# The end of an fp32 encoder kernel: last weight tile in four blocks, last output half by fp32 products, final norm by halves of the columns

## The reference, cut to what matters

```python
def _rmsnorm(x, g):
    xf = x.astype(jnp.float32)
    y = xf * lax.rsqrt(jnp.mean(xf * xf, axis=-1, keepdims=True) + RMS_EPS)
    return (y * g.astype(jnp.float32)).astype(x.dtype)

def _moe(h, router, w_gate_up, w_down):
    ...
    for e in range(N_EXPERTS):
        y = y + gate_full[..., e:e + 1] * _swiglu(h, w_gate_up[e], w_down[e])
    return y
```

## Time and profile before

| | us |
|---|---|
| median of 3 runs | 1533.2 |
| the three runs | 1531.36, 1533.20, 1534.36 |
| profiled execution: span, first to last instruction | 1531.6 |
| from the landing of the last weight tile to the end of the span | 22.8 |

### The profile page before, as it was taken

The page is one execution under the profiler, slowest core; times in us unless marked ns, Lnnn a source line. Parts: engine busy times, 40 slices in busy tenths (PEclk is TensorE's granted clock), DMA queues, the critical chain, the costliest instruction groups (busy, mean ns, idle before and its releaser), DMA issues.

```text
span 1531.6 us, 19275 instructions
## 1 busy us (share of the span) xinstructions
PE 1487.0 (97%) x7570; PEld 1216.4 (79%) x7570; DVE 1166.2 (76%) x1009; ACT 996.8 (65%) x861; POOL 151.5 (10%) x130
## 2 busy tenths in 40 slices
PE   8999999999989999999999999999999999999995
PEld 6888888899979987788777788777888777887783
DVE  5555445455455455999899988899898999898996
ACT  5443434343363446777798777888776888776994
POOL 0000000013034022400000300000300002000000
PEclk9999999999999999999999999999999999999998
DMA  9655555566507642699999999999999999999994
GB/s 335 210 192 167 191 175 182 192 194 219 189 32 221 219 165 83 227 410 407 362 408 422 399 409 411 386 411 418 401 414 404 385 411 417 403 402 406 386 394 167
DMA packets 151119, 468.31 MB, mean 306 GB/s; under 512 B 9792, under 2 KB 15936, under 8 KB 138480
## 3 DMA queue, kind: packets, MB, share of 16 engines
q1 hardware_dynamic: 144720, 453.93, 78.8%
q0 software_dynamic: 2816, 9.96, 2.3%
q10 hardware_dynamic: 3488, 3.13, 0.7%
HBM read 459.62 MB, written 7.37 MB: 305 GB/s over the span
## 4 chain that ended last, share of the span: by engine, by line
PE 77%; DVE 15%; ACT 3%; issue 2%; DMA 1%; SPq 1%; DVEq 0%; ACTq 0%
DVE wlo L405 10%; PE bS L424 6%; PE bS L423 6%; PE bS L425 6%; PE bY L423 6%; PE bY L424 6%; PE bY L425 6%; PE bG L423 4%; PE bU L423 4%; PE bU L424 4%; PE bU L425 4%; PE bG L424 4%; PE bG L425 4%; ACT whi L399 2%; DVE wlo_more L405 2%
## 5 line engine op out<-in xcount | busy, mean ns | idle before, releaser
L405 DVE TENSOR_TENSOR wlo<-raw,whi 128x2048 fp32r<-128x2048 f32 x368 | 834.8, 2295 | 187.3 <-ACT whi L399 186.5
L399 ACT ACTIVATE whi<-raw 128x2048 fp32r<-128x2048 f32 x368 | 699.6, 1914 | 262.3 <-PE bS L425 136.3
L405 DVE TENSOR_TENSOR wlo_more<-raw_more,whi 128x2048 fp32r<-128x2048 f32 x58 | 131.8, 2286 | 9.8 <-ACT whi L399 9.6
L399 ACT ACTIVATE whi<-raw_more 128x2048 fp32r<-128x2048 f32 x58 | 110.3, 1915 | 21.9 <-PE bS L425 9.1
L1010 PE MATMUL bY<-whi,hTh 128*128 128x512 f32 x224 | 91.4, 408 | 7.8 <-DVE wlo L405 5.2
L423 PE MATMUL bY<-whi,hTh 128*128 128x512 f32 x224 | 89.7, 401 | 0.0
L424 PE MATMUL bY<-whi,hTl 128*128 128x512 f32 x224 | 88.9, 397 | 0.0
L553 POOL TENSOR_TENSOR bias<-biasrev,band 128x256 f32<-128x256 f32 x32 | 33.2, 1038 | 510.5 <-DMA biasrev<-toeplitz 381.8
L1010 PE MATMUL bS<-whi,eTh 128*128 128x512 f32 x192 | 76.2, 397 | 0.0
L423 PE MATMUL bS<-whi,eTh 128*128 128x512 f32 x192 | 76.2, 397 | 0.0
L424 PE MATMUL bS<-whi,eTl 128*128 128x512 f32 x192 | 76.1, 396 | 0.0
(11 more groups left out here) (476 smaller groups left out, 3376.3 us busy)
## 6 DMA issues: line engine op xcount, KB each, us to landing
raw<-in_m_w_gate_up_dram SPq DMA_DIRECT2D x188, 1024.0 KB, 13.8
raw<-in_m_w_down_dram SPq DMA_DIRECT2D x90, 1024.0 KB, 13.7
raw<-in_b_w_in_dram SPq DMA_DIRECT2D x36, 1024.0 KB, 5.1
raw_more<-in_m_w_gate_up_dram SPq DMA_DIRECT2D x36, 1024.0 KB, 15.0
raw<-in_f_w_gate_up_dram SPq DMA_DIRECT2D x28, 1024.0 KB, 5.1
raw_more<-in_m_w_down_dram SPq DMA_DIRECT2D x22, 1024.0 KB, 13.5
raw<-in_f_w_down_dram SPq DMA_DIRECT2D x14, 1024.0 KB, 5.0
raw<-in_a_w_out_dram SPq DMA_DIRECT2D x4, 1024.0 KB, 16.0
```

Of the source, the lines that this page charges most:

```text
L399: nc.scalar.activation(whi[:, h], raw_of(r), ACT.Copy).then_inc(hi_done, 1)
L405: nc.vector.tensor_tensor(wlo_of(r), raw_of(r), whi[:, h].bitcast(F32), ALU.subtract).then_inc(lo_done, 1)
```

## The change

- The last tile of the last item is loaded by four DMAs (one for each block of 512 columns), made high by four activations (`last_tile_hi`) and low by four subtractions (`last_tile_lo`), and PE waits block by block.
- The right half of the output isn't cut in two: ACT copies it in fp32 to `y_out` (`y_right`), and PE spreads it by one fp32 product for each block of 128 rows (`spread_right`), into banks U and G. There is a semaphore for each.
- On DVE and ACT the overflow loop comes ahead of everything that needs the right half. PE comes to it behind `spread_right`.
- The final norm goes by halves of the columns: ACT sums all squares, in four activations of 512 columns, the left ones ahead of the right ones. DVE multiplies block 1 by the gain, in two halves (`gained`); POOL has no part in it. The last scaling goes by halves on ACT and DVE.
- The output leaves by three DMAs: two of 128 rows by 2 KB on SP (block 0) and one of 128 rows by 4 KB on ACT (block 1).
- The overflow item itself is written anew in the same way.

```diff
+        last_full, last_hi, last_lo = [sem(f"last_full{b}") for b in range(3)], sem("last_hi"), sem("last_lo")
+        right_psum, left_gained = sem("right_psum"), sem("left_gained")
+        def store(engine, tb, cols):
+            engine.dma_start(out[0].rearrange("(m t a) d -> t a m d", t=NT, a=2)[tb][:, :, cols],
+                             hn[:, tb, cols]).then_inc(stored, 16)
+                if by_half and t == FFN_TILES - 1:
+                    for b in range(4):
+                        sp.dma_start(dst[:, b * 512:b * 512 + 512], src[:, b]).then_inc(
+                            last_full[b] if b < 3 else full_count(t_all, n)[0], 16)
+                    return
...
-            for a in range(4):
-                if a % 2 == 0:
-                    sp.wait_ge(out_ready[a // 2], 1)
-                sp.dma_start(out[0].rearrange("(m a) d -> a m d", a=4)[a],
-                             hn[a % 2 * 64:a % 2 * 64 + 64, a // 2, :]).then_inc(stored, 16)
-            sp.wait_ge(stored, 64)
+            for h in range(2):
+                sp.wait_ge(out_ready[0], h + 1)
+                store(sp, 0, slice(h * 512, h * 512 + 512))
+            sp.wait_ge(stored, 48)
...
-            pool.wait_ge(x_final, 1)
-            pool.wait_ge(c_in[C_GAIN4], 16)
-            nc.gpsimd.tensor_tensor(hn[:, 1], x[:, 1], gain[:, 1], ALU.mult).then_inc(hn_done, 1)
...
-            def spread(h, banks):
+            def spread_left():
 
                 for part, y in enumerate((yh, yl)):
                     for tb in (1, 0):
-                        mm = pe.matmul(banks[tb][:], selT[:, tb], y[:, h * 512:h * 512 + 512], start=part == 0, stop=part == 1)
+                        mm = pe.matmul((S0, S1)[tb][:], selT[:, tb], y[:, 0:512], start=part == 0, stop=part == 1)
                 mm.then_inc(sc_psum, 1)
+
+            def spread_right():
+
+                for tb in (1, 0):
+                    pe.matmul((G, U)[tb][:], selT[:, tb].bitcast(F32), y_out[:, 512:D], start=True, stop=True
+                              ).then_inc(right_psum, 1)
...
-                    tile_ready(T_MOE + t, n)
+                    if not by_half or t < FFN_TILES - 1:
+                        tile_ready(T_MOE + t, n)
                     for s, blk, kb, stop in blocks_of(t, by_half):
+                        if by_half and t == FFN_TILES - 1 and blk < 3:
+                            pe.wait_ge(last_lo, blk + 1)
+                        if by_half and t == FFN_TILES - 1 and blk == 3:
+                            tile_ready(T_MOE + t, n)
...
-                spread(0, (S0, S1))
+                spread_left()
 
             half_item(E - 1, LOW - 1, last_amid, last_spread, by_half=True)
-            pe.wait_ge(x_added, 1)
-            pe.wait_ge(y_lo, 2)
-            spread(1, (S0, S1))
+            pe.wait_ge(y_hi, 2 * E)
+            spread_right()
...
-            def y_split(n, h, tiles=FFN_TILES):
+            def y_left(n, tiles=FFN_TILES):
 
                 act.wait_ge(tile_used, count(n, FFN_TILES, T_MOE + tiles))
-                copy(yh[:, h * 512:h * 512 + 512], (Y0, Y1)[h][:], y_hi)
+                copy(yh[:, 0:512], Y0[:], y_hi)
+
+            def y_right(n):
+
+                act.wait_ge(tile_used, count(n, FFN_TILES, T_MOE + FFN_TILES))
+                copy(y_out[:, 512:D], Y1[:], y_hi)
+
+            def last_tile_hi(t, n):
+
+                r, h = slots(t, n)
+                act.wait_ge(tile_used, used_count(t, n, HI))
+                for b in range(4):
+                    act.wait_ge(*((last_full[b], 16) if b < 3 else full_count(t, n)))
+                    sl = slice(b * 512, b * 512 + 512)
+                    nc.scalar.activation(whi[:, h, sl], raw_of(r)[:, sl], ACT.Copy).then_inc(last_hi if b < 3 else hi_done, 1)
...
-                        if not by_half or t + CUT < FFN_TILES:
+                        if by_half and t + CUT == FFN_TILES - 1:
+                            last_tile_hi(T_MOE + t + CUT, n)
+                        elif not by_half or t + CUT < FFN_TILES:
                             make_hi(act, T_MOE + t + CUT, n)
...
-                y_split(E - 1, h, DOWN + DT * h + DT)
+                    y_left(E - 1, DOWN + DT)
 
             half_item(E - 1, LOW - 1, last_split, by_half=True, amid=last_amid)
             with act.Fori(0, OVER) as m:
                 with act.If(m < m_last):
+                    y_right((m, 1, E - 1))
...
-            root(4)
+            y_right((m_last, 1, E - 1))
+            nc.scalar.activation(small[:, 9:10], ident[:, 0:1], ACT.Sqrt)
+            act.wait_ge(x_added, m_last * 2 + 1)
+            for tb in (1, 0):
+                last = nc.scalar.activation(squares[:, tb, 0:512], x[:, tb, 0:512], ACT.Square, accum_out=small[:, 12 + tb:13 + tb])
+            last.then_inc(sq_done, 1)
+            for i, tb in enumerate((1, 0)):
+                act.wait_ge(x_final, i + 1)
+                last = nc.scalar.activation(squares[:, tb, 512:D], x[:, tb, 512:D], ACT.Square, accum_out=ss[:, tb:tb + 1])
+            last.then_inc(sq_done, 1)
+            act.wait_ge(ms_done, 5)
+            nc.scalar.activation(std, ms, ACT.Sqrt).then_inc(std_done, 1)
             act.wait_ge(rstd_done, 5)
-            act.wait_ge(hn_done, 5)
-            copy(hn[:, 1], hn[:, 1], out_ready[1], scale=rstd[:, 1:2])
+            for h in range(2):
+                act.wait_ge(left_gained, h + 1)
+                sl = slice(h * 512, h * 512 + 512)
+                copy(hn[:, 1, sl], hn[:, 1, sl], out_ready[1], scale=rstd[:, 1:2])
+            act.wait_ge(out_ready[1], 2)
+            store(act, 1, slice(0, D))
...
-            def y_low(n, h):
-
-                dve.wait_ge(y_hi, count(n, 2, h + 1))
-                sl = slice(h * 512, h * 512 + 512)
-                lo(yl[:, sl], (Y0, Y1)[h][:], yh[:, sl], y_lo)
-
-            def add_item(h, banks, psum, added, column):
+            def y_low(n):
+
+                dve.wait_ge(y_hi, count(n, 2, 1))
+                lo(yl[:, 0:512], Y0[:], yh[:, 0:512], y_lo)
+
+            def last_tile_lo(t, n):
+
+                r, h = slots(t, n)
+                for b in range(4):
+                    dve.wait_ge(*((last_hi, b + 1) if b < 3 else (hi_done, t + FFN_TILES * n + 1)))
+                    sl = slice(b * 512, b * 512 + 512)
+                    nc.vector.tensor_tensor(wlo_of(r)[:, sl], raw_of(r)[:, sl], whi[:, h, sl].bitcast(F32),
+                                            ALU.subtract).then_inc(last_lo if b < 3 else lo_done, 1)
+
+            def add_right(tb, column):
+
+                sl = x[:, tb, 512:D]
+                return nc.vector.scalar_tensor_tensor(sl, (G, U)[tb][:], gate_item[:, tb, column], sl, ALU.mult, ALU.add)
+
+            def add_left(psum, added, column):
 
                 dve.wait_ge(sc_psum, psum)
                 if added is not None:
                     dve.wait_ge(x_added, added)
-                for tb in range(NT):
-                    sl = x[:, tb, h * 512:h * 512 + 512]
-                    last = nc.vector.scalar_tensor_tensor(sl, banks[tb][:], gate_item[:, tb, column], sl, ALU.mult, ALU.add)
+                for tb in (1, 0):
+                    sl = x[:, tb, 0:512]
+                    last = nc.vector.scalar_tensor_tensor(sl, (S0, S1)[tb][:], gate_item[:, tb, column], sl, ALU.mult, ALU.add)
                 last.then_inc(x_added, 1)
...
+                        if by_half and t + CUT == FFN_TILES - 1:
+                            last_tile_lo(T_MOE + t + CUT, n)
+                        elif not by_half or t + CUT < FFN_TILES:
                             make_lo(dve, T_MOE + t + CUT, n)
...
                 if by_half:
-                    y_cut(0)
+                    y_cut()
                 else:
                     late()
                 ahead(*range(DOWN + 7, DOWN + 12))
                 if by_half:
                     late()
                 ahead(DOWN + 12, DOWN + 13)
-                if by_half:
-                    y_cut(1)
...
-            dve.wait_ge(sc_psum, m_last * 2 + 2)
+            def gained(h):
+                sl = slice(h * 512, h * 512 + 512)
+                nc.vector.tensor_tensor(hn[:, 1, sl], x[:, 1, sl], gain[:, 1, sl], ALU.mult).then_inc(left_gained, 1)
+
+            dve.wait_ge(c_in[C_GAIN4], 16)
             dve.wait_ge(x_added, m_last * 2 + 1)
-            for tb in (1, 0):
-                sl = x[:, tb, 512:D]
-                nc.vector.scalar_tensor_tensor(sl, (S0, S1)[tb][:], gate_item[:, tb, one((m_last, 1, E - 1))], sl,
-                                               ALU.mult, ALU.add).then_inc(x_final, 1)
+            gained(0)
+            for i, tb in enumerate((1, 0)):
+                dve.wait_ge(right_psum, m_last * 2 + (i + 1))
+                add_right(tb, one((m_last, 1, E - 1))).then_inc(x_final, 1)
+            dve.wait_ge(x_final, 1)
+            gained(1)
+            dve.wait_ge(sq_done, 5)
```

(43 more changed lines are left out.)

12 lines of the change are left out of this document (5 added, 7 removed).

## The result

| | before | changed |
|---|---|---|
| median, us | 1532.28 (4 runs, 1530.71 to 1534.36) | 1545.28 (4 runs, 1543.09 to 1548.34) |
| ratio, 95% | | 1.0085 [1.0068, 1.0101] |
| profiled execution, its own time | | 1544.12 |
| its span | 1531.6 | 1542.2 |

What follows compares the result with a forecast made beforehand. It took the one-at-a-time relay of engines behind the last weight tile, 22.8 us with no engine at its limit, as the bound; the span's end moves from 1531.6 to 1526.3, so 1533.2 - 5.3 = 1527.9 us, range 1525.9 to 1530.3.

Steps and rivals of the forecast that it cites:

- step 6: Output stores: first store 4.75 us earlier in all, then 5.4 us to the end, bounds 4.4 and 5.97.
- C: Rival at the last tile's four loads: fixed DMA times add up, slower, 1536.6 to 1542 us in full; chance 0.04.
- aside on 4.4 us for 1 MB: Stores: the skill's 2.0 us plus bytes at 436 GB/s, putting the end an estimated 0.6 us earlier.
- Step 1: Last weight tile in four blocks: PE's gap closes and its last product starts 0.67 us earlier.
- Step 2: Right-half cut: subtraction gone, fp32 products at 1.03 us and 0.86 more for the second.
- rival A: fp32 products of the spread: clock falls, or a wait replaces the loop; 1529.6 us; chance 0.18.
- Step 3: DVE's overflow loop: about 1.3 us of its 3.1 leave the chain; it ends at 1514.7, or about 1513.5.
- Step 4: DVE's additions: right ones start at 1516.4 and 1517.25, 0.75 us each; right gain product costs nothing beside ACT's squares.
- Step 5: Final norm's squares: ACT's own queue sets the end, squares 0.70 us apart; scaling starts 4.17 us earlier.
- B: Rival at the last blocks' semaphore or ACT's overflow loop: late or not covered, 1530.5 us; chance 0.12.

Runs made afterwards that it cites:

- e2: The kernel before with its four stores of 64 rows replaced by two of 2 x 64 rows on SP; 1550.37 us, ratio 1.0114.
- e3: The changed kernel with ACT's store issued by SP instead, same shape; 1546.2 us.
- e1: The changed kernel with each of its three stores issued as two of 64 rows; 1528.69 us, ratio 0.9974 to the kernel before.
- e12: The kernel before with block 1's two stores issued by ACT instead of SP; 1533.17 us in one run.
- e11: e5 with all four stores on SP, none on ACT; 1529.57 us, ratio 0.9975 to the kernel before.
- e5: e1 with four stores of 64 whole rows, two each on SP and ACT, and ACT's root-table load ahead of the right-half copy; 1528.88 us, ratio 0.997.
- e6: e1 with the last weight tile whole again: one DMA, one activation, one subtraction, one wait; 1529.02 us.
- e8: e1 with the right half spread again as high and low fp32r parts, two products a block, with DVE's subtraction; 1527.5 us.
- e7: e1 with DVE's overflow loop held back until ACT's copy of the right half; 1529.12 us.
- e9: e1 with the old final norm: DVE sums block 0's squares, POOL multiplies by the gain, scaling in 1024 columns, whole rows stored; 1528.81 us.
- e4: e1 with each store's 64 rows addressed as 4 x 16, output rows in another order; 1537.62 us, ratio 1.003 to the kernel before.

## Why the prediction was wrong

**The step that failed is step 6**, the stores. It took the 5.97 us from first store to end over as an upper end, "if the 1 MB of data is the limit", and put 5.4 in its place. It counted stores, issues and bytes and never looked at the shape that `store` gives a DMA. The code of the change had it in sight: `[tb][:, :, cols]` on `t a m d` leaves a dimension of two on the outside, where the old loop indexed `a` and left 64. That term measured 23.62 (e2: 23.53, e3: 23.66), 18.2 above the 5.4 taken and 17.65 above the upper end. Of the rivals, none held it: C, the slower one, put the loss at the four loads of the last tile and at their fixed times, and those came on time.

With the shape mended (e1) the term is 6.36, still above the 4.4 to 5.97 of the prediction. Its reason, that issues come closer together and leave from two queues, was wrong in sign: e12 puts two queues into the kernel before and loses 0.70, e11 takes them away and gains 0.77 against e5. The step's aside on 4.4 us for 1 MB would put the end 1.0 us earlier than the 5.4 taken does, not 0.6; the shortest measured is e11's 5.90.

**Step 1** (0.67) was right: 0.65 between the last products (6.65 to 6.00), 0.70 at the end by e6.

**Step 2** was right as a size, the first right addition at 8.38 against 8.25. Its fp32 products took 1.13 and 1.02 against 1.03, the second 0.96 behind the first against 0.86, with a granted clock of 1.00 from 1513 to 1515.2, so rival A didn't occur. But by e8 the fp32 products are worth nothing in e1: what they save the right additions, 0.32 and 0.15, is covered by ACT's queue of squares. In e5, where ACT waits for the first of these additions, they may count; no run shows it.

**Step 3** was right that the loop leaves the chain, and too cautious about when. Jumps of DVE's loop in the changed kernel (durations in ns, first and last start):

```profile
L2086 DVEq COMPARE_BRANCH  x4: 63/66/73, 1508.4 to 1511.0; - x4
```

The loop began 0.1 us after the first of the four low parts (1508.27), with the other three and both left additions, which stand ahead of it, still to start, and it was over soon after the last of them ended (1510.76). On the clock of the kernel before it would be over near 1513.2; the forecast took 1514.7 with three instructions allowed to stand, and 1513.5 where all five may stand. The queue of 8 for VectorE (the Trainium skill, Advanced Engine Details and Errata, Engine Queue Depths) speaks for the latter. This row agrees as far as it goes: it shows room for five, not where the room ends. By e7 it costs 2.12 to have the loop, and the left gain product behind it, wait for ACT's copy.

**Step 4** was right: additions of 0.75, 0.85 apart, and the right gain product covered by ACT's squares. **Step 5** was right in kind, ACT unbroken from table load to last square, and 0.26 better in size (scaling 4.43 earlier instead of 4.17), since the squares followed each other by 0.61 and not 0.70. By e9 the new norm and its scaling by halves are worth 2.06 at the first store.

Rivals A and B left no trace: every wait that they name is short or absent. The parts ahead of the stores gave 4.96 us up to the first store (17.48 to 12.52, forecast 4.75), and e1 and e11 keep most of it: e1 loses some to its longer stores, e11 to a first store that waits for whole rows. Their ends lie 4.62 and 4.69 before that of the kernel before in the traces, and 3.65 and 4.0 in the medians, whose intervals (2.6 to 5.4 us for e1, 2.3 to 5.5 for e11) hold both figures.

## What to carry to other kernels

Before a DMA's time is taken from another of the same size, compare the shapes on both sides, outermost dimension first: a row order folded into the pattern of one large DMA can leave it on two engines, and two DMAs in its place, each with 64 rows outside, remove that. Where several engines work one behind the other at the end, the parts of this change held up well, each priced by its own row; the term that was written down in one line, because nothing seemed to change in it, is the one to look at again. A part that is priced by its own gain (the fp32 product here) can be worth nothing once another engine's queue binds.

## What the runs showed of the hardware

- DMA engines by outer dimension of the destination: 2 gives a mean share of 0.13 and 48 GB/s, 4 gives 0.24 and 81 GB/s, 64 gives 0.79 and 210 to 233 GB/s. The small packets beside the rows are 2, 4 and 16 a store. In their steady parts two engines carry 52 GB/s and four 101. Three stores on two queues share the same two engines (23.62 against 23.66 on one queue).
- Four stores of 256 KB: 5.90 to 5.98 us from first issue to end on SP alone, 6.67 on SP and ACT.
- POOL's gain product (two inputs of 1024 columns) delays DVE's work beside it: a sum of squares of 1024 columns takes 2.71 to 2.83 instead of 1.23, a scaling 3.04 instead of 1.28, each ending 1.08 or 1.09 after POOL's, while POOL takes 2.34 to 2.36 in all.
- An fp32 product of 128 x 128 by 512 columns took 1.02 to 1.13, and two of them are 0.96 apart.
- The issue of a store can itself take long: one of e3's three took 3342 ns, against 522 for the shortest; the longest was 2204 in e4, 1537 in e1 and 952 in the kernel before.
